# An eleventh 2 MB buffer for expert weights, and the first weight chunk placed between the halves of the first input

## The chip, the cores and the metric

The kernel runs on one core of a Trainium2 chip. The metric is the device time of one execution in microseconds (us), as a median over runs. The engines of the core are named as in the profile: PE (matmul) with its weight load PEld, DVE (vector), ACT (scalar), POOL, and SP, which here issues nearly all DMAs. "PE psum L434" is the matmul helper `mm`, which nearly all products go through.

## What is computed

A stack of three layers on 256 tokens of width 1024, batch 1, all in float32. The part that the change touches is the first layer:

```python
h = _layer_norm(x, ln_in_g, ln_in_b)                 # the first input
mix = _token_mixer(h, w_in, ...)                     # gm_v, gm_u, gates, delta rule, w_pa, w_pb, w_o
h = _layer_norm(ALPHA * h + mix, ln1_g, ln1_b)
ffn = _hier_moe(h, w_rg, b_rg, w_re, b_re, w1, w3, w2)
h = _layer_norm(ALPHA * h + ffn, ln2_g, ln2_b)

def expert_block(xb, e):                             # 32 experts, top 2 of each token
    return (silu(xb @ w1[e]) * (xb @ w3[e])) @ w2[e] # w1, w3: 1024 x 512; w2: 512 x 1024
```

Each of the 96 expert matrices is 2 MB in float32. After the experts come two layers of attention and gated feed-forward (`second_block`), whose code is the same in both kernels.

## The kernel before

**The mixer (from 0 us to about 382 us).** Weights arrive as 2 MB items in slots 0 to 3 of a ring in SBUF. Most products are made exact to about float32 from three passes in a faster format. ACT copies a half of the item (a "chunk", 128x2048) rounded into `mix_hi` (line 1245), DVE subtracts to get the low part (`slot_lo`, line 1808), and PE multiplies high by high, high by low and low by high. The input h is split the same way into `h_hi` (ACT, line 1221) and `h_lo` (DVE, line 1844), in four pieces of two 128-row blocks each. In the first 30 us PE transposes the normalised input (line 540), DVE scales it (line 1839), both are split, and then two products follow on PE: `ab_rows` (24 small products of h with `wab`, 16 rows wide), and `gm_v`, whose first weight item is used in two chunks: chunk 0 needs the blocks 0 to 3 of h, chunk 1 the blocks 4 to 7. PE works through an order written by hand: all 24 products of `ab_rows`, then chunk 0, then chunk 1.

**The delta rule (about 229 us to 310 us).** Between the projections lies a stretch of very small matmuls (64x64), several hundred in a row. SP loads `w_pb` items 0 and 1 ahead of it, at 212 and 229.7 us, and `w_o` at 288.6 and 329.8 us. Between them it waits.

**The experts (about 383 us to 843 us).** PE takes the experts in 16 pairs. A pair reads six items in the order w1, w3 (first expert), w1, w3 (second expert), w2, w2. They are numbered here from 0 to 95 in this order; the table `BUFFER_SLOTS` says where each of ten buffers lies: six are the ring slots, the entries `None` are four pairs of free pages (`spare`). Item u goes to buffer u modulo 10. SP first fills the ten buffers as the places come free (lines 2626 and 2633), then for each u waits until PE has read item u and issues the load of item u + 10 into the same buffer (`consumed` and `load_next`; lines 2652 for pages and 2654 for the ring). That runs as a loop of 30 items taken twice, and 26 items written out. The weights of the next stage (`e_lora`, then three `e_in`, `mla_up`, `e_out`) follow in ring slots in the order of `RING_ORDER`, each when its slot was read for the last time.

**The instruction streams.** PE's expert code is written out, some 11,000 matmuls in the whole program. The profile shows its instructions coming in by DMA on a queue of their own (q8, 79 packets, 1.29 MB).

## Time and profile before

| | us |
|---|---|
| median of 3 runs (lowest to highest) | 1443.21 (1442.02 to 1443.51) |
| the profiled execution, its own time | 1444.03 |
| its span from first to last instruction | 1442.2 |
| PE busy, share of the span | 1391.2, 96% |
| PE waiting for expert weights (DMA ring<-in_w) | 3.7, four times |
| PE waiting for nothing that shows ("issue") | 8.7, four times |

The span is cut by what PE does; PE's busy time counts matmuls as they are pipelined, so a stretch that reads 100% busy can still differ in pace. What matters is therefore when an instruction starts, which the timeline gives, and what ended the idle time ahead of it, which stands in square brackets behind a row. A DMA is known by the time from its issue on SP to its landing.

### The profile page before, as it was taken

What the parts mean: (1) busy time and instruction counts of PE and PEld (TensorE: products, weight loads), DVE (VectorE), ACT (ScalarE), POOL (GpSimd) and SP (SyncE); (2) the same over time, 40 slices, a digit from 0 to 9 for tenths busy, and PEclk for the clock granted to TensorE, in tenths of its full rate; (3) what the DMA queues carried; (4) which work ended last, traced back from release to release, by engine and by line L of the source; (5) the groups of instructions that cost most, each with busy time, mean ns of one, the idle gap of its engine ahead of it and who ended that gap; (6) DMA issues with size and microseconds to landing.
All of it is one profiled execution on the core that took longest, in us unless ns stands there. A gap on an engine that the chain in (4) does not pass through costs nothing.

```text
span 1442.2 us, 25893 instructions
## 1 busy us (share of the span) xinstructions
PE 1391.2 (96%) x11102; PEld 1137.4 (79%) x11102; DVE 703.5 (49%) x1086; ACT 543.1 (38%) x851; POOL 18.6 (1%) x15
## 2 busy tenths in 40 slices
PE   7999999999999999999999979999999998999997
PEld 5999999979666666666656548879999986899996
DVE  6766896346611111111111056866555668755554
ACT  3555773345111111111111144654433456633343
POOL 0000004000000000000000000000000000000000
PEclk9999999899999999999999989999999999999999
DMA  9534432018879999999999991244554631455420
GB/s 388 228 118 176 182 146 85 2 60 339 343 318 426 423 427 423 427 423 427 425 426 424 426 398 67 92 170 178 191 198 165 233 132 45 154 200 187 174 87 30
DMA packets 31473, 351.98 MB, mean 244 GB/s; under 512 B 3088, under 2 KB 3344, under 8 KB 4880
## 3 DMA queue, kind: packets, MB, share of 16 engines
q1 hardware_dynamic: 31232, 349.49, 60.2%
q8 instruction: 79, 1.29, 0.4%
q10 hardware_dynamic: 144, 1.05, 0.2%
q14 instruction: 18, 0.15, 0.0%
HBM read 349.48 MB, written 1.05 MB: 243 GB/s over the span
## 4 chain that ended last, share of the span: by engine, by line
PE 85%; DVE 8%; DMA 3%; ACT 2%; issue 2%; DVEq 0%; ACTq 0%
PE psum L434 83%; DMA ring<-in_w 3%; PE psum L540 1%; DVE slot_lo L1808 1%; ACT pages L1221 1%; PE psum L841 1%; DVE pages L2324 1%; DVE pages L2357 1%; DVE tiny L1756 0%; ACT w_hi L1245 0%; DVE pages L1988 0%; DVE pages L2328 0%; DVE pages L1778 0%; DVE pages L2417 0%; DVE pages L1769 0%
## 5 line engine op out<-in xcount | busy, mean ns | idle before, releaser
L434 PE MATMUL psum<-pages 64*64 64x64 f32 (+11 forms) x3280 | 317.3, 311 | 7.8 <-ACT pages L1221 2.6
L434 PEld LDWEIGHTS psum<-pages 128*64 128x64 f32 (+4 forms) x3280 | 225.4, 151 | 85.1 <-issue 48.0
L434 PE MATMUL psum<-ring,pages 128*64 128x256 f32 (+1 forms) x1556 | 210.2, 423 | 4.2 <-DMA ring<-in_w 3.7
L434 PE MATMUL psum<-x_hi,gu_hi 128*128 128x256 f32 x704 | 199.8, 284 | 0.1
L434 PE MATMUL psum<-x_hi,gu_lo 128*128 128x256 f32 x704 | 199.2, 283 | 0.0
L434 PE MATMUL psum<-x_lo,gu_hi 128*128 128x256 f32 x704 | 199.2, 283 | 0.0
L434 PEld LDWEIGHTS psum<-ring,pages 128*64 128x64 f32 x1556 | 110.8, 137 | 89.3 <-issue 40.9
L434 PEld LDWEIGHTS psum<-x_hi,gu_hi 128*128 128x128 f32 x704 | 134.9, 192 | 2.7 <-issue 0.6
L434 PEld LDWEIGHTS psum<-x_lo,gu_hi 128*128 128x128 f32 x704 | 134.9, 192 | 1.5
L434 PEld LDWEIGHTS psum<-x_hi,gu_lo 128*128 128x128 f32 x704 | 134.9, 192 | 0.0
L1808 DVE TENSOR_TENSOR slot_lo<-ring,mix_hi 128x2048 fp32r<-128x2048 f32 x44 | 100.7, 2290 | 59.1 <-ACT mix_hi L1245 59.0
L2245 DVE SCALAR_TENSOR_TENSOR y_lo<-psum,pages,y_hi 128x512 fp32r<-128x512 f32 x32 | 24.0, 751 | 177.8 <-ACT y_hi L1467 177.8
L434 PE MATMUL psum<-h_hi,mix_hi 128*128 128x256 f32 x448 | 110.6, 287 | 0.0
L434 PE MATMUL psum<-h_lo,mix_hi 128*128 128x256 f32 x448 | 109.5, 284 | 0.0
L2256 DVE TENSOR_TENSOR pages<-pages,psum 128x256 f32<-128x256 f32 x32 | 13.5, 421 | 194.9 <-ACT pages L1476 194.9
L2374 DVE TENSOR_TENSOR gu_lo<-ring,gu_hi 128x2048 fp32r<-128x2048 f32 x44 | 100.9, 2292 | 1.4 <-ACT gu_hi L1575 0.2
L1245 ACT ACTIVATE mix_hi<-ring 128x2048 fp32r<-128x2048 f32 x44 | 84.0, 1912 | 41.3 <-PE psum L434 39.8
L1588 ACT ACTIVATE pages<-pages 128x256 f32<-128x256 f32 x44 | 18.5, 421 | 209.8 <-DVE pages L2391 209.8
L1476 ACT ACTIVATE pages<-psum 128x256 f32<-128x256 f32 x32 | 12.3, 383 | 205.1 <-PE psum L434 205.1
L434 PEld LDWEIGHTS psum<-h_hi,mix_hi 128*128 128x128 f32 x448 | 86.6, 193 | 0.6 <-issue 0.5
L2391 DVE TENSOR_TENSOR pages<-psum,pages 128x256 f32<-128x256 f32 x44 | 18.7, 425 | 139.9 <-PE psum L434 139.9
L434 PEld LDWEIGHTS psum<-h_lo,mix_hi 128*128 128x128 f32 x448 | 86.6, 193 | 0.1
(233 smaller groups left out, 2050.7 us busy)
## 6 DMA issues: line engine op xcount, KB each, us to landing
ring<-in_w SPq DMA_DIRECT2D x58, 2048.0 KB, 25.3
pages<-in_w SPq DMA_DIRECT2D x38, 2048.0 KB, 25.8
ring<-in_ffn SPq DMA_DIRECT2D x44, 1536.0 KB, 6.3
ring<-in_w_in SPq DMA_DIRECT2D x16, 2048.0 KB, 8.5
ring<-in_e_in SPq DMA_DIRECT2D x3, 2048.0 KB, 38.5
ring<-in_w_pa SPq DMA_DIRECT2D x2, 2048.0 KB, 7.7
ring<-in_w_pb SPq DMA_DIRECT2D x2, 2048.0 KB, 8.0
ring<-in_w_o SPq DMA_DIRECT2D x2, 2048.0 KB, 7.4
```

Source lines behind the costliest of these rows:

```text
L434: return pe.matmul(o, lhsT, rhs, start=start, stop=stop, skip_group_check=True)
L540: last = pe.transpose(o[:, j * P:(j + 1) * P], s, ident)
L841: last = pe.transpose(psum[:, 2 + r, c * P:(c + 1) * P], act[:, r, c * P:(c + 1) * P], ident)
L1221: st.do(act_e.activation(o, i, func, **kw), name)
L1245: act_e.activation(high[:, 0:size], slot(n)[:, c * size:(c + 1) * size], ACT.Copy).then_inc(S("w_high"), 1)
L1588: act_e.activation(silu_buf[:, j % 3, :], silu_buf[:, j % 3, :], ACT.Silu).then_inc(S(f"{nm}_silu"), 1)
L1808: ve.tensor_tensor(slot_low[slot_no(n)][:, sl], slot(n)[:, sl], high[:, 0:size], ALU.subtract).then_inc(S("w_split"), 1)
L2245: return ve.scalar_tensor_tensor(y_part["lo"][:, r, :], psum[:, 2 + r, :], gate, y_part["hi"][:, r, :], ALU.mult, ALU.subtract)
L2324: do(ve.scalar_tensor_tensor(e[:, h2, :], bias, slope(g), v[:, 0:SPAN], ALU.mult, ALU.add), f"{sec}s{g}")
L2357: do(ve.tensor_tensor(e[:, :, sl], e[:, :, sl], z[:, :, b].unsqueeze(2).broadcast_to([P, 2, size]), ALU.mult), f"{sec}_probs" if b else None)
L2374: ve.tensor_tensor(gu_part["lo"][j % 2], slot(item_no[(nm, 0)] + j)[:, 0:gu_size], gu_part["hi"][j % 2], ALU.subtract).then_inc(S("gu_spli ...
L2391: ve.tensor_tensor(silu_buf[:, j3, :], psum[:, j3, 0:T], rstd_rows, ALU.mult).then_inc(S("gate_scaled"), 1)
```

## The change

It has three parts. (1) The ring gets a seventh slot, `EXTRA`. It is buffer 0 of now eleven, item 0 is loaded into it right behind `w_pb` item 1, without any wait, and item u + 11 replaces item u. The loop on SP is written out. The space comes from `dynamic_dma_scratch_size=1024` (16384 bytes per partition before). (2) `RING_ORDER` follows the order in which the eleven-buffer scheme lets the ring slots go. (3) At the start PE does half of `ab_rows`, then chunk 0 of `gm_v`, the other half, chunk 1; ACT and DVE split chunk 0 between the second and the third piece of h.

```diff
-BUFFER_SLOTS = (5, None, 2, 3, None, 0, 1, 4, None, None)
+EXTRA = 6
+BUFFER_SLOTS = (EXTRA, 5, None, 2, 3, None, 0, 1, 4, None, None)
-RING_ORDER = (1, 4, 5, 2, 3, 0)
+RING_ORDER = (4, 5, 2, 3, 0, 1)
...
-        ring = sb("ring", [P, SLOTS * SLOT])
+        ring = sb("ring", [P, (SLOTS + 1) * SLOT])
...
-            o = take("ab_rows", 6)
-            for k in range(KD):
-                if k % 2 == 0:
-                    pe.wait_ge(*V("ln_in_low", k // 2 + 1))
-                for n, (wp, xp) in enumerate(PARTS):
-                    last = mm(...)
-            give(last, "ab_rows")
-            project_tokens("gm_v", [("gm_v", 0), ("gm_v", 1)])
+            take("ab_rows", 6)
+            row_products(0)
+            tokens_half("gm_v", 0, ("gm_v", 0), 0, mix_highs[0], h_part)
+            row_products(1)
+            tokens_half("gm_v", 0, ("gm_v", 0), 1, mix_highs[1], h_part)
+            for c in range(2):
+                tokens_half("gm_v", 1, ("gm_v", 1), c, mix_highs[c], h_part)
...
                 act(h_part["hi"][:, sl, :], h_in[:, sl, :], ACT.Copy, "ln_in_high")
+                if i == 1:
+                    split_high(1)
...
             for n, (name, i) in enumerate(items[:moe_first]):
                 load(n, name, i)
+                if phases >= 2 and (name, i) == ("w_pb", 1):
+                    sp.dma_start(ring_slot(EXTRA), first_of(BUFFER_SLOTS.index(EXTRA))).then_inc(landed[EXTRA], 16)
...
-                rounds = (3 * EXPERTS - BUFFERS) // (6 * ROUND)
-                with sp.Fori(0, rounds) as it:
-                    for u in range(6 * ROUND):
-                        consumed(it, u)
-                        load_next(it, u)
-                for u in range(3 * EXPERTS - BUFFERS - 6 * ROUND * rounds):
-                    consumed(rounds, u)
-                    load_next(rounds, u)
+                for u in range(3 * EXPERTS - BUFFERS):
+                    consumed(u)
+                    load_next(u)
...
-    nc = bacc.Bacc("TRN2", target_bir_lowering=False, num_devices=1)
+    nc = bacc.Bacc("TRN2", target_bir_lowering=False, num_devices=1, dynamic_dma_scratch_size=1024)
```

DVE at the start, before: L1829 normalises the input, L1839 scales a transposed piece, L1844 makes its low part, L1808 the low part of a weight chunk.

```order
L1839 TENSOR_SCALAR pages<-psum,consts 128x256 x4
L1844 TENSOR_TENSOR h_lo<-pages,h_hi 128x512
L1839 TENSOR_SCALAR pages<-psum,consts 128x256 x2
L1844 TENSOR_TENSOR h_lo<-pages,h_hi 128x512
L1839 TENSOR_SCALAR pages<-psum,consts 128x256 x2
L1844 TENSOR_TENSOR h_lo<-pages,h_hi 128x512 x2
L1808 TENSOR_TENSOR slot_lo_61<-ring,mix_hi 128x2048 x2
```

DVE at the start, of the changed kernel, where L1852, L1859 and L1821 are the same three statements.

```order
L1852 TENSOR_SCALAR pages<-psum,consts 128x256 x4
L1859 TENSOR_TENSOR h_lo<-pages,h_hi 128x512 x2
L1852 TENSOR_SCALAR pages<-psum,consts 128x256 x4
L1821 TENSOR_TENSOR slot_lo_61<-ring,mix_hi 128x2048
L1859 TENSOR_TENSOR h_lo<-pages,h_hi 128x512 x2
L1821 TENSOR_TENSOR slot_lo_61<-ring,mix_hi 128x2048
```

The low part of chunk 0 moved ahead of the low parts of the last two pieces of h, and the second piece's low part ahead of the third piece's scaling.

PE at the same place, as a piece of the difference: the rows with a plus stood ahead of all weight products and now follow chunk 0 (the three shown, four times).

```order
 L434 MATMUL psum<-mix_hi,h_lo 128x512
 L434 MATMUL psum<-slot_lo_61,h_hi 128x512 x8
+L434 MATMUL psum<-h_hi,wab_hi 16x256
+L434 MATMUL psum<-h_lo,wab_hi 16x256
+L434 MATMUL psum<-h_hi,wab_lo 16x256
```

Half of the small products now stand behind the sixteen high and eight low products of chunk 0.

SP from the delta rule into the first expert loads, before.

```order
L2602 DMA ring<-in_w_pb 128x4096 x2
L2602 DMA ring<-in_w_o 128x4096 x2
L2616 DMA pages<-in_router 128x864
L2617 DMA pages<-in_ln 128x2048
L2633 DMA ring<-in_w 128x4096
L2626 DMA pages<-in_w 128x4096
```

SP at the same place, of the changed kernel; L2623 is the load into `EXTRA`.

```order
L2617 DMA ring<-in_w_pb 128x4096 x2
L2623 DMA ring<-in_w 128x4096
L2617 DMA ring<-in_w_o 128x4096 x2
L2634 DMA pages<-in_router 128x864
L2635 DMA pages<-in_ln 128x2048
L2652 DMA ring<-in_w 128x4096
L2645 DMA pages<-in_w 128x4096
```

One 2 MB load was added between `w_pb` and `w_o`; every later expert load stands at its old place and carries the next item.

## Rows read from the trace of the kernel before

**Rows 1.** The page: busy tenths of the DMA engines in 40 slices

```profile
DMA  9534432018879999999999991244554631455420
```

**Rows 2.** Busy time by stretch: us, PE, PEld, DVE, ACT, POOL, PEclk, DMA share, GB/s

```profile
398.20:404.20 6.00, 6.00 (x57) 4.69 (x58) 1.10 (x5) 2.16 (x3) 0.00 (x0) 1.00 0.01 3
450.00:600.00 150.00, 150.00 (x1169) 92.21 (x1168) 19.16 (x39) 22.55 (x45) 0.00 (x0) 1.00 1.01 425
```

**Rows 3.** Timeline of PE, experts: start us, us, engine, line, op, operands, count [idle <-releaser]

```profile
755.80 7.08 PE L434 MATMUL psum<-pages 128*64 128x256 f32 x64
...
769.73 0.73 PE L434 MATMUL psum<-y_hi,spots 64*128 64x512 f32 x4
...
783.15 3.62 PE L434 MATMUL psum<-pages 128*64 128x256 f32 x32
...
799.15 0.73 PE L434 MATMUL psum<-y_hi,spots 64*128 64x512 f32 x4
...
812.57 3.62 PE L434 MATMUL psum<-ring,pages 128*64 128x256 f32 x32
...
820.62 3.67 PE L434 MATMUL psum<-ring,pages 128*64 128x256 f32 x32 [0.97 <-DMA ring<-in_w]
825.42 3.67 PE L434 MATMUL psum<-ring,pages 128*64 128x256 f32 x32 [1.12 <-DMA ring<-in_w]
829.02 0.73 PE L434 MATMUL psum<-y_hi,spots 64*128 64x512 f32 x4
```

**Rows 4.** Timeline of PE, the start

```profile
13.02 0.37 PE L434 MATMUL psum<-h_hi,wab_hi 128*16 128x256 f32 x1
...
15.40 0.28 PE L434 MATMUL psum<-h_hi,wab_lo 128*16 128x256 f32 x1
...
16.07 0.28 PE L434 MATMUL psum<-h_lo,wab_hi 128*16 128x256 f32 x1
16.19 0.28 PE L434 MATMUL psum<-h_hi,wab_lo 128*16 128x256 f32 x1
...
17.81 0.50 PE L434 MATMUL psum<-mix_hi,h_hi 128*128 128x512 f32 x1 [0.20 <-ACT mix_hi L1245]
...
21.57 1.98 PE L434 MATMUL psum<-slot_lo,h_hi 128*128 128x512 f32 x8
23.39 0.39 PE L434 MATMUL psum<-mix_hi,h_hi 128*128 128x512 f32 x1
```

**Rows 5.** Timeline of DVE, the start

```profile
12.20 0.68 DVE L1844 TENSOR_TENSOR h_lo<-pages,h_hi 128x512 fp32r<-128x512 f32 x1
12.79 0.99 DVE L1839 TENSOR_SCALAR pages<-psum,consts 128x256 f32<-128x256 f32 x2
...
17.79 2.29 DVE L1808 TENSOR_TENSOR slot_lo<-ring,mix_hi 128x2048 fp32r<-128x2048 f32 x1 [1.11 <-ACT mix_hi L1245]
```

**Rows 6.** Timeline of ACT, the start

```profile
12.31 0.63 ACT L1221 ACTIVATE h_hi<-pages 128x512 fp32r<-128x512 f32 x1 [0.27 <-DVE pages L1839]
...
15.86 3.71 ACT L1245 ACTIVATE mix_hi<-ring 128x2048 fp32r<-128x2048 f32 x2
```

**Rows 7.** Line L2602 in the window 2.5 to 3.0 us: the first weight item, issued at 2.60

```profile
DMA to landing us min/median/max: 9.3/9.3/9.3
```

**Rows 8.** Timeline of PE, small matmuls of the delta rule

```profile
238.51 15.47 PE L434 MATMUL psum<-pages 64*64 64x64 f32 x507 [1.36 <-issue]
```

**Rows 9.** DMA issue of the window 229.7 to 230.0 us: KB, us to landing

```profile
ring<-in_w_pb SPq DMA_DIRECT2D x1, 2048.0 KB, 8.5
```

**Rows 10.** DMA packets by queue, window 236.2 to 236.3 us: packets, MB, share

```profile
q8 instruction: 1, 0.02, 59.6%
```

**Rows 11.** DMA packets by queue, window 239.6 to 239.8 us

```profile
q8 instruction: 1, 0.02, 38.2%
```

**Rows 12.** DMA packets by queue, window 239.6 to 255.5 us

```profile
q8 instruction: 5, 0.08, 2.5%
```

**Rows 13.** DMA issue of the window 798.7 to 799.0 us: KB, us to landing

```profile
ring<-in_e_lora SPq DMA_DIRECT2D x1, 1792.0 KB, 40.9
```

More of the change, by code:

```diff
@@ L254, in build @@
         free = [S(f"bank{b}_free") for b in range(8)]
-        landed = [S(f"slot{s}_landed") for s in range(SLOTS)]
+        landed = [S(f"slot{s}_landed") for s in range(SLOTS + 1)]
         by_page = pages[:].rearrange("p (n c) -> p n c", c=PAGE)
-        spare = {1: by_page[:, 5:7, :], 4: by_page[:, 2:5:2, :], 8: by_page[:, 1:4:2, :], 9: by_page[:, 7:13:5, :]}
+        spare = {2: by_page[:, 5:7, :], 5: by_page[:, 2:5:2, :], 9: by_page[:, 1:4:2, :], 10: by_page[:, 7:13:5, :]}
         spare_landed = {b: S(f"spare{b}_landed") for b in spare}
@@ L574, in _, with row_products @@
             pe.wait_ge(*V("wab_split", 1))
-            o = take("ab_rows", 6)
-            for k in range(KD):
-                if k % 2 == 0:
-                    pe.wait_ge(*V("ln_in_low", k // 2 + 1))
-                for n, (wp, xp) in enumerate(PARTS):
-                    last = mm(o[0:16, 0:T], wab_part[wp][:, k, :], h_part[xp][:, k, :], k == 0 and n == 0, k == KD - 1 and n == 2)
-            give(last, "ab_rows")
-            project_tokens("gm_v", [("gm_v", 0), ("gm_v", 1)])
+            take("ab_rows", 6)
+            def row_products(half):
+                o = bank_of("ab_rows")
+                for k in range(half * KD // 2, (half + 1) * KD // 2):
+                    if k % 2 == 0:
+                        pe.wait_ge(*V("ln_in_low", k // 2 + 1))
+                    for n, (wp, xp) in enumerate(PARTS):
+                        last = mm(o[0:16, 0:T], wab_part[wp][:, k, :], h_part[xp][:, k, :], k == 0 and n == 0, k == KD - 1 and n == 2)
+                if half:
+                    give(last, "ab_rows")
+            row_products(0)
[4 more added lines that the diff above has]
+                tokens_half("gm_v", 1, ("gm_v", 1), c, mix_highs[c], h_part)
             pe.wait_ge(*evacuated("ab_rows"))
@@ L1834, in _ @@
                "wab_split")
-            for i in range(5):
-                if i < 4:
+            for first in (0, 2):
+                for i in (first, first + 1):
                     v = await_full(ve, f"ln_in_T{i}")
@@ L1840, in _ @@
                                             ALU.mult, ALU.add), f"ln_in_T{i}" if k % 2 else None)
-                if i:
-                    sl = slice(2 * i - 2, 2 * i)
-                    ve.wait_ge(*V("ln_in_high", i))
+                if first:
+                    split_low(1)
+                for i in (first, first + 1):
+                    sl = slice(2 * i, 2 * i + 2)
+                    ve.wait_ge(*V("ln_in_high", i + 1))
                     do(ve.tensor_tensor(h_part["lo"][:, sl, :], h_in[:, sl, :], h_part["hi"][:, sl, :], ALU.subtract), "ln_in_low")
@@ L2618, in _ @@
             if phases >= 2:
-                first_of = lambda i: io[LOADS[i % 6]][2 * (i // 6) + LOAD_OF[i % 6]]
                 halves_of = lambda src: src.rearrange("p (n c) -> p n c", c=PAGE)
-                spare_free = {1: V("h_split", 8), 4: (full[place["w_pb3"][0]], place["w_pb3"][1]),
-                              8: (full[place["w_o3"][0]], place["w_o3"][1]), 9: V("ln1_tokens", 4)}
+                spare_free = {2: V("h_split", 8), 5: (full[place["w_pb3"][0]], place["w_pb3"][1]),
+                              9: (full[place["w_o3"][0]], place["w_o3"][1]), 10: V("ln1_tokens", 4)}
                 for i, s in enumerate(BUFFER_SLOTS):
+                    if s == EXTRA:
+                        continue
                     if s is None:
@@ L2634, in _, with consumed, load_next @@
                 base = place["moe_base"]
[L2636 removed]
+                def consumed(u):
                     x = u % 6
                     if x in (0, 2):
[L2640 removed]
+                        sp.wait_ge(*V("w1_read", 2 * (u // 6) + x // 2 + 1))
                     elif x < 4:
[L2642 removed]
+                        sp.wait_ge(full[x // 2], u // 6 + base[x // 2] + 1)
                     else:
[L2644 to L2650 removed]
+                        sp.wait_ge(full[x - 2], 2 * (u // 6) + base[x - 2] + 2)
+                def load_next(u):
+                    b, src = u % BUFFERS, first_of(u + BUFFERS)
                     if b in spare:
```

10 lines of the change are left out of this document (1 added, 9 removed).

## The prediction

> **What bounds the kernel now.** I read the page first, then the expert stage in the windows and in PE's timeline, then the start, then the quiet stretch into which the new load falls. The page shows that the DMA engines are nearly full at the very start and from the tenth slice on (about 325 us) to the twenty-fourth, and idle elsewhere [rows 1]. In the expert stage they move 425 GB/s at a share of 1.01, so they can give no more [rows 2]. A pair of experts needs six items, 12.58 MB, which take 29.6 us at that rate. PE needs less: the h products of one pair start at 755.80 and those of the next at 783.15, 27.35 us later [rows 3]. So the weights fall behind PE by 2.2 us with each pair, and the ten items that lie ready at the start are a lead that is used up. It lasts until the last two pairs. There PE waits four times, 0.97 and 1.12 us in the last pair [rows 3] and twice in the pair ahead of it. The true loss is read from starts, since each stop also costs a little refill: from the first h product to the first scatter it is 13.93 us in an undisturbed pair (755.80 to 769.73), 16.00 in the next to last (783.15 to 799.15) and 16.45 in the last (812.57 to 829.02) [rows 3]. Excess: 2.07 + 2.52 = **4.6 us**. Outside the experts PE works nearly without a gap, so time comes only from gaps in PE's row.
>
> **Part 1, the eleventh buffer, as a lead.** Item u + 11 is now issued at the moment at which item u + 10 was, since SP waits for the same read of item u; and the places in which the first fill goes come free in the same order. From 398.2 to 404.2 us the DMA engines stand still, the ten buffers being full, and then they never stop [rows 2]; that gap stays. So in the saturated stretch each item lands when its predecessor did: 2.097 MB / 425 GB/s = 4.93 us earlier; the two waits of the last pair end 4.80 us apart (820.62 and 825.42), and I go by that [rows 3]. Item 93 is the tightest. It lands when item 92 did, at about 820.6. Without any waits PE would want it at 825.42 less the delay gathered by then, 2.07 + 2.52 less the small rest behind it, about 4.5, so at 820.9. It is there with 0.3 us to spare, the other three with more than 1.5. All four waits go, and nothing else is late next: the two w2 items of the last pair have 1.5 us or more. **-4.55 us**, taken between -3.2 (item 93 still late by up to 1.3 us, should the stream run 0.3% slower over 430 us) and -4.6. The loads of the next stage: `RING_ORDER` gives `e_in` and `mla_up` ring slots that PE lets go up to one product block later than before, but `e_lora`, issued at 798.7, landed only 40.9 us later [rows 13], the queue ahead of it being that long. They wait in the queue, not for their slot, and the queue is 4.9 us earlier while PE is 4.55 us earlier. Cost nothing. The written-out loop issues the same DMAs on an SP that only waits. Nothing.
>
> **Part 2, the load into `EXTRA`.** It is free of any wait and needed 150 us later. Its DMA queue is empty until `w_o` at 288.6. But PE is not indifferent here. `w_pb` item 1 is issued at 229.73 and lands 8.5 us later, at 238.3 [rows 9]; behind it come 507 matmuls of 64x64 in 15.47 us, 30.5 ns each, ahead of which PE stood for 1.36 us and waited for nothing that shows [rows 8]. What shows beside it is an instruction packet of 16 KB, which starts at 236.2 to 236.3, while `w_pb` flows [rows 10]. The next one starts at 239.6 to 239.8, five of them lie in 15.9 us, so one each 3.9 us when the data queue is quiet, and PE has no such gap then [rows 11, 12]. Take 3.9 us of PE's own time back from 239.7, with the 1.36 us of standing between: the packet at 236.2 was due at about 239.7 - 3.9 - 1.36 = 234.4. It came 1.8 us late, behind data packets, and PE has about 0.45 us of slack for it. So a small-matmul stretch stalls by 1.36 us when an instruction packet meets a 2 MB transfer. Now the transfer of `EXTRA` follows at once and keeps the engines full for 4.9 us more, to about 242. The packet of 239.7 falls into it. The nearest row is the stall itself: once more **+1.4 us**. A little more is likely, because the packet of 236.2 came when its engine had just run out of `w_pb` data, and now there is more behind: half a data packet, 0.3 us. Together **+1.7 us**. Bounds: 0 if a fetch passes the data (then the first stall would be of another cause), and 4.9 us if a fetch waits for the whole second transfer. The path there is PE's own, so what is lost stays lost.
>
> The Trainium skill bears on this twice. "Runtime: NRT & Kernel Launch", Instruction fetch mechanics, says that each engine refills 256 instructions (16 KiB) at a time by its own DMA queue and calls the cost mostly hidden; the trace agrees on the size (q8) and not on the rest, as the 1.36 us show. By that page the term would be 0 and the time 1437.9. "DMA: Bandwidth & Descriptors", Queues, rings and completion order, says that a DMA engine goes round its rings but drains some 9 to 17 descriptors from one before it moves on. If the upper figure held, the fetch would wait through both transfers; that is rival C below, worked out from rows.
>
> **Part 3, the start.** PE needs 4.79 us from the first `ab_rows` product (13.02) to the first weight product (17.81) [rows 4]. The first twelve products start 0.22 us apart (13.02 to 15.40), the later ones 0.12 (16.07, 16.19) [rows 4]. Without waits that is 12 x 0.21 + 12 x 0.12 = 3.9 us; the rest, **0.9 us**, is waiting for pieces of h and for ACT's copy. After: ACT has the second `h_hi` at 12.94, and the weights landed at 2.60 + 9.3 = 11.9 [rows 6, 7], so chunk 0's copy takes 12.94 to 14.8 (half of 3.71). DVE does the two first low parts to 13.7 (0.68 each), then four scalings to 15.6 (0.99 a pair), then chunk 0's low part to 17.9 (2.29), the last low parts to 19.2 and chunk 1's to 21.4 [rows 5]. PE: twelve products to 15.5; chunk 0's sixteen high products from 15.5 to 19.3 (17.81 to 21.57 took 3.76) and eight low ones to 21.1 (1.82) [rows 4]; twelve products, for which h is ready since 19.2, to 22.5; then chunk 1. Before, the same work was done at 23.39 [rows 4]. No wait is left, the closest being the copy at 14.8 for 15.5. **-0.9 us**; bounds -0.9 (there is no more waiting to remove) and 0 (if PE's quick pace, which begins at 15.3, comes later with the new order). DVE and ACT are ahead of their old place afterwards, so nothing is pushed on.
>
> **Sum.** -4.55 + 1.7 - 0.9 = -3.75 us. On the profiled execution 1444.03 - 3.75 = 1440.3 (span 1442.2 to 1438.4); it is 0.8 us above the median, so the median should be 1443.2 - 3.75 = **1439.5**. About 0.2%, 2.9 us, is what a measurement of this kernel can tell from no change; the bound is 1440.3.
>
> **Rivals.** A, the forecast: 1438.7 to 1440.9 with its small spreads. B, the second stall does not come or is under 0.5 us: 1443.2 - 5.45 + 0.25 = 1438.0. For it: in the expert stage, where the DMA is always full, no such stall shows; against: there the matmuls are ten times as long, so a block of instructions lasts some 16 us. C, the fetch waits for all of `EXTRA`: +4.9 in place of 1.7, 1442.7. Against it: the packet at 236.2 waited for 1.8 us of the 4.9 of a transfer. D, the lead is not worth its whole: item 93 late, or the start brings nothing: -3.2 + 1.7 - 0.3, 1441.4. E, the other side, slower: the scratch of 1024 bytes holds the DMA queue's descriptors, and a sixteenth of it lets only one transfer be under way at a time. Then each of 85 streamed items would take its lone time, 8.5 us [rows 9], where it takes 4.93; the price is 85 x 3.6 = 300 us, less the lead of 36, some 1700 us. It decides as soon as fewer than two transfers fit; with two or more the stream stays at 425 GB/s and costs nothing. Against it: all data packets are marked hardware_dynamic. The Trainium skill, the same DMA page, SWDGE vs HWDGE vs iDMA, places only the software rings in that scratch; no run here shows it yet.
>
> **How the numbers follow.** Chances: A 0.52, B 0.20, C 0.12, D 0.13, E 0.03. The forecast is A's 1439.5. Its own range is 1438.7 to 1440.9; with B below, C and D above, I go from 1437.6 to 1442.4, which leaves out E and the far ends of B and C. Faster by over 0.2% (under 1440.3): three quarters of A and all of B, some 0.60. Within 0.2%: the rest of A, C and D, 0.37. Slower: 0.03.
>
> **What would show it.** In the profile after: no PE wait on ring<-in_w (else part 1's lead is short); the last two pairs 13.9 us each from h to scatter; PE's first product of chunk 1 at about 22.5 in place of 23.39; an "issue" wait near 237 and a second one near 241 to 243, where before there was one, the second of 1.0 to 2.0 us. If the second is missing, B; if one of them is 5 us, C. Landings of expert weights that are 7 us or more apart would be E. The sum fails most easily in the size of part 2, whose two bounds are 4.9 us apart.

## The result and the profile after

The changed kernel takes **1436.75 us** (median of 5 runs, 1436.45 to 1438.11). The kernel before, run beside it, takes 1443.51 us (median of 5, 1442.02 to 1445.24). The ratio is 0.9956, 95% interval 0.9945 to 0.9967. That is 6.8 us faster, where 3.75 us was forecast, and 0.85 us below the lower end of the range. Two more measurements of the same changed kernel (experiments, below) gave ratios of 0.9957 and 0.9963. Over all its 15 runs the changed kernel has a mean of 1437.5 us, and the kernel before over the 62 runs that stood beside these and the other kernels one of 1443.1 us: **5.6 us**, give or take 0.6. So the sign is certain, and the size is best taken from the many runs: the first medians, 6.8 us apart, are partly luck. The profiled execution of the changed kernel took 1436.71 us, with a span of 1434.9 us.

I go through the profile after in the order of the prediction. **The experts** first. Timeline of PE, changed kernel (start us, us, engine, line, operation, operands, count):

```profile
767.18 0.73 PE L434 MATMUL psum<-y_hi,spots 64*128 64x512 f32 x4
...
794.51 0.73 PE L434 MATMUL psum<-y_hi,spots 64*128 64x512 f32 x4
...
807.93 3.62 PE L434 MATMUL psum<-pages 128*64 128x256 f32 x32
...
821.84 0.73 PE L434 MATMUL psum<-y_hi,spots 64*128 64x512 f32 x4
```

The brackets "<-DMA ring<-in_w" of [rows 3] are gone, and the last pair takes 13.91 us from its first h product to its first scatter (807.93 to 821.84), as an undisturbed one did before. The last three scatters start 27.33 us apart (767.18, 794.51, 821.84), which is PE's own pace for a pair, where the last pair of before took 29.87 (799.15 to 829.02) and the one ahead of it 29.42. From the first scatter to the last it is 410.02 us, and it was 414.66. The stream itself is what it was, 426 GB/s for 425 in [rows 2]:

```profile
450.00:600.00 150.00, 150.00 (x1174) 92.13 (x1172) 19.17 (x39) 21.41 (x43) 0.00 (x0) 1.00 1.01 426
```

**The small products** of the delta rule, the place of [rows 8]. Timeline of PE, changed kernel:

```profile
228.27 7.52 PE L434 MATMUL psum<-pages 64*64 64x64 f32 x246
237.42 3.94 PE L434 MATMUL psum<-pages 64*64 64x64 f32 x127 [1.63 <-issue]
242.63 16.32 PE L434 MATMUL psum<-pages 64*64 64x64 f32 x523 [1.27 <-issue]
258.88 1.12 PE L434 MATMUL psum<-consts 128*128 128x512 f32 x2
```

Of the kernel before, the first product of the same stretch and the first one behind it:

```profile
229.63 7.52 PE L434 MATMUL psum<-pages 64*64 64x64 f32 x246
...
258.60 1.12 PE L434 MATMUL psum<-consts 128*128 128x512 f32 x2
```

There are two stalls for which nothing is waited, 1.63 and 1.27 us, where before there was one of 1.36 (and a small one of 0.17 further on). The second one is new. The brackets are not the whole loss. By starts, the 896 products take 28.97 us before (229.63 to 258.60) and 30.61 after (228.27 to 258.88): 1.64 us more, where the brackets differ by 1.37. An instruction packet shows beside each: q8 in the windows 234.9 to 235.1 and 240.2 to 240.4 of the changed kernel (packets, MB, share), to be laid beside [rows 10, 11].

```profile
q8 instruction: 1, 0.02, 29.8%
```

```profile
q8 instruction: 1, 0.02, 30.4%
```

Both fall into the two transfers, issued at 228.4 and 228.7. Issues of the window 228 to 229 us, KB and us to landing, which answer to [rows 9]:

```profile
ring<-in_w_pb SPq DMA_DIRECT2D x1, 2048.0 KB, 8.7
ring<-in_w SPq DMA_DIRECT2D x1, 2048.0 KB, 13.0
```

**The start**, the place of [rows 4 to 6]. Timelines of PE, and of DVE, changed kernel:

```profile
12.93 0.37 PE L434 MATMUL psum<-h_hi,wab_hi 128*16 128x256 f32 x1
...
14.59 0.34 PE L434 MATMUL psum<-h_hi,wab_lo 128*16 128x256 f32 x1
14.77 0.28 PE L434 MATMUL psum<-h_hi,wab_hi 128*16 128x256 f32 x1
...
15.12 0.40 PE L434 MATMUL psum<-mix_hi,h_hi 128*128 128x512 f32 x1
...
20.61 0.28 PE L434 MATMUL psum<-h_hi,wab_hi 128*16 128x256 f32 x1
...
22.01 0.40 PE L434 MATMUL psum<-mix_hi,h_hi 128*128 128x512 f32 x1
```

```profile
15.30 2.28 DVE L1821 TENSOR_TENSOR slot_lo<-ring,mix_hi 128x2048 fp32r<-128x2048 f32 x1
17.50 1.29 DVE L1859 TENSOR_TENSOR h_lo<-pages,h_hi 128x512 fp32r<-128x512 f32 x2
18.71 2.29 DVE L1821 TENSOR_TENSOR slot_lo<-ring,mix_hi 128x2048 fp32r<-128x2048 f32 x1
```

No bracket is left in PE's row from its first product on. Its first product of chunk 1 starts at 22.01; it was 23.39. DVE's low parts are done at 17.6, 18.8 and 21.0, each ahead of its reader.

**What I had not looked for: the granted clock.** Windows of both kernels around two short stretches (us, PE, PEld, DVE, ACT, POOL, PEclk, DMA share, GB/s). Of the kernel before:

```profile
262.00:284.00 22.00, 20.57 (x182) 19.74 (x179) 6.67 (x8) 8.43 (x18) 0.00 (x0) 0.77 0.01 1
383.00:400.00 17.00, 17.00 (x100) 12.36 (x97) 8.37 (x56) 2.43 (x6) 2.31 (x3) 0.90 0.77 323
```

Of the changed kernel:

```profile
262.00:284.00 22.00, 20.57 (x197) 19.84 (x192) 6.96 (x8) 9.48 (x21) 0.00 (x0) 0.84 0.01 1
383.00:400.00 17.00, 17.00 (x111) 12.44 (x112) 9.09 (x59) 3.06 (x6) 2.31 (x3) 1.00 0.70 295
```

The seventh number behind the window is the granted clock, 1.00 being 2.4 GHz. A mean of 0.77 over 22 us is 10.2 us at half of it, 1.2 GHz (2 x 0.23 x 22); 0.84 is 6.8 us, and 0.90 over 17 us is 3.4 us. So the profiled execution of before ran 3.4 us longer at 1.2 GHz near 268 us, and 3.4 us near 387 us where the changed one had none. PE's timeline prices them. The 40 router products, before and after:

```profile
383.39 8.87 PE L434 MATMUL psum<-pages 128*128 128x36 f32 x40
```

```profile
382.32 7.17 PE L434 MATMUL psum<-pages 128*128 128x36 f32 x40
```

Near 268 us, 32 products of the delta rule's second part, before and after, and the first product with a low part behind them:

```profile
268.51 7.35 PE L434 MATMUL psum<-pages 64*128 64x128 f32 x32 [1.43 <-ACT pages L1221]
...
280.74 2.08 PE L434 MATMUL psum<-h_hi,slot_lo 128*128 128x256 f32 x16
```

```profile
268.79 5.62 PE L434 MATMUL psum<-pages 64*128 64x128 f32 x32 [1.43 <-ACT pages L1232]
...
279.67 2.08 PE L434 MATMUL psum<-h_hi,slot_lo 128*128 128x256 f32 x16
```

The same work takes 12.23 us in the one (268.51 to 280.74) and 10.88 in the other. What PE did before its clock fell: near 268 it ran 128 small products and stood 1.43 us for ACT (the clock fell during that wait before, at 267.9, and behind it after, at 270.7); near 387 it had stood 1.38 and 0.23 us for DVE between transposes, and it did so in both kernels, though the clock fell in one alone.

**The account** of the two profiled executions, between marks of PE and SP that both traces have. The parts add up to the difference of the spans, 1442.2 - 1434.9 = 7.3 us.

| stretch | before | after | difference |
|---|---|---|---|
| to the issue of `w_pb` item 1 (start moved) | 229.73 | 228.37 | -1.36 |
| the 896 small products, first start to the next product's | 28.97 | 30.61 | +1.64 |
| rest of the way to the issue of `w_o` item 1 (clock near 268) | 71.11 | 69.76 | -1.35 |
| from there to the first scatter (clock near 387) | 84.55 | 83.08 | -1.47 |
| first to last scatter (experts) | 414.66 | 410.02 | -4.64 |
| behind the last scatter | 613.22 | 613.08 | -0.14 |

Three rows are the prediction's three terms, and they sum to -4.36. Two more, -2.8 us together, lie where the clock differs, and the first of them is just what the work near 268 lost above (12.23 - 10.88 = 1.35).

### The profile page after: what moved, and what is told of

Its sections match the earlier page's. It is cut to its first block, busy times and chain, and to the rows that moved or that the text cites. A ratio compares the mean times of both kernels' runs of the same rounds, so it can differ in the third digit from the quotient of the medians.

```text
span 1434.9 us, 25774 instructions
## 1 busy us (share of the span) xinstructions
PE 1386.7 (97%) x11102; PEld 1135.5 (79%) x11102; DVE 703.5 (49%) x1086; ACT 543.0 (38%) x851; POOL 18.6 (1%) x15
## 4 chain that ended last, share of the span: by engine, by line
PE 89%; DVE 7%; ACT 2%; issue 1%; DMA 0%; DVEq 0%; ACTq 0%
PE psum L434 86%; PE psum L540 2%; DVE slot_lo L1821 1%; PE psum L852 1%; ACT pages L1232 1%; DVE pages L2339 1%; DVE pages L2372 1%; DVE tiny L1769 0%; DVE pages L2003 0%; DVE pages L2343 0%; DVE pages L1791 0%; DVE pages L2432 0%; DVE pages L1782 0%; DVE pages L2382 0%; ACT w_hi L1256 0%
## 5 line engine op out<-in xcount | busy, mean ns | idle before, releaser
L434 PE MATMUL psum<-pages 64*64 64x64 f32 (+9 forms) x3184 | 299.9, 305 | 8.8 <-issue 2.9
L434 PEld LDWEIGHTS psum<-pages 128*64 128x64 f32 (+3 forms) x3184 | 216.8, 151 | 78.3 <-issue 44.2
L434 PE MATMUL psum<-ring,pages 128*64 128x256 f32 (+1 forms) x1652 | 223.2, 424 | 0.9 <-ACT pages L1492 0.9
L434 PEld LDWEIGHTS psum<-ring,pages 128*64 128x64 f32 x1652 | 117.1, 137 | 92.0 <-issue 42.6
L1821 DVE TENSOR_TENSOR slot_lo<-ring,mix_hi 128x2048 fp32r<-128x2048 f32 x44 | 100.8, 2290 | 57.4 <-ACT mix_hi L1256 57.3
L1489 ACT ACTIVATE pages<-psum 128x256 f32<-128x256 f32 x32 | 12.3, 383 | 200.4 <-PE psum L434 200.4
```

The source lines that it names most:

```text
L434: return pe.matmul(o, lhsT, rhs, start=start, stop=stop, skip_group_check=True)
L1821: ve.tensor_tensor(slot_low[slot_no(n)][:, sl], slot(n)[:, sl], high[:, 0:size], ALU.subtract).then_inc(S("w_split"), 1)
```

## Theories, and the experiments

Theory: the three parts are worth about -1.4 us (the start), -4.6 (the buffer) and +1.3 to +1.7 (its load) each by itself and add up to between -4.7 and -4.3. What is measured beyond that is the clock's stretches at 1.2 GHz, which vary between executions of one kernel. Rivals: (1) the rest of the gain is a fourth effect of the change (the scratch of 1024 bytes, the written-out loop, `RING_ORDER`); (2) the stall among the small products is of that place in the code, and the transfer only stands beside it; (3) the missing stretch at 387 us is the change's doing.

### The start alone

The reorder of `ab_rows` and `gm_v` and of DVE's and ACT's pieces, with ten buffers:

```diff
-            project_tokens("gm_v", [("gm_v", 0), ("gm_v", 1)])
+            row_products(0)
+            tokens_half("gm_v", 0, ("gm_v", 0), 0, mix_highs[0], h_part)
+            row_products(1)
...
```

> The kernel before with the new order at the start alone (ten buffers, old loop on SP). Theory (the start is worth what PE's row shows, and the rest of the gain beyond the sum came from half-clock windows): PE's first w_pb release moves from 229.7 to about 228.4 us, the four DMA waits at the end of the experts stay (excess 4.6 us over undisturbed pairs), one issue wait of about 1.4 us near 236, total about -1.4 us, 1442.1. Rival (the start also brings the other 3 us, for instance because PE reaches the later stretches at a luckier moment for the clock): the windows of granted clock 0.5 near 268 and 387 us shrink or go here too and the total is -3 to -4 us.

Measured: 1441.64 us (median of 11), ratio 0.9987 (0.9978 to 0.9996). `w_pb` item 1 is issued at 228.09, the four DMA waits of the last two pairs are there (0.53, 1.12, 1.06 and 1.14 us), and there is one stall by issue, 1.73 us. So the start is worth 1.3 to 1.8 us of time (difference of medians, of means), where I had 0.9; the reason stands in the next section. And this kernel, with ten buffers, has no stretch at 1.2 GHz near 387 us. Rival 3 loses its ground as far as the buffer is meant: the stretch goes without it too.

### The buffer alone

The eleventh buffer, its load behind `w_pb` item 1, the new `RING_ORDER`, the written-out loop and the scratch of 1024 bytes, with the old start:

```diff
-BUFFER_SLOTS = (5, None, 2, 3, None, 0, 1, 4, None, None)
+EXTRA = 6
+BUFFER_SLOTS = (EXTRA, 5, None, 2, 3, None, 0, 1, 4, None, None)
...
```

> The changed kernel with the old order at the start. Theory: no DMA wait in the experts, each pair 27.33 us (-4.6 us), two issue waits in the small matmuls, the first about 1.5 and the second about 1.3 us later (+1.5 us), total about -3.1 us, 1440.4, give or take 1.5 us of half-clock windows whose place is chance. Rival (the buffer part gave the surplus of 3 us, by shortening the half-clock windows near 268 and 387 us): -5 to -6 us, and these windows are shorter here than in the kernel before.

Measured: 1438.86 us (median of 5), ratio 0.9966 (0.9952 to 0.9979). No DMA wait in the experts; first to last scatter 410.02 us. The two stalls are there:

```profile
229.61 7.52 PE L434 MATMUL psum<-pages 64*64 64x64 f32 x246
238.21 3.94 PE L434 MATMUL psum<-pages 64*64 64x64 f32 x127 [1.08 <-issue]
243.69 15.71 PE L434 MATMUL psum<-pages 64*64 64x64 f32 x523 [1.54 <-issue]
```

The lead and the second stall belong to the buffer, and neither needs the new start. The time is 4.1 us lower by medians (5.1 by means). Theory had 3.1 and the rival 5 to 6, so the time alone favours neither, and it is more than the -4.6 + 1.3 = -3.3 of its rows; this profiled execution also lacks the stretch near 387 us and one near 940 us, while its 10.2 us near 268 are not shorter.

### `EXTRA` loaded one item earlier

The changed kernel with the load of `EXTRA` behind the earlier `w_pb` item, issued near 210 us, where PE does larger products:

```diff
-                if phases >= 2 and (name, i) == ("w_pb", 1):
+                if phases >= 2 and (name, i) == ("w_pb", 0):
```

> The changed kernel with the load into the seventh slot issued behind the first w_pb item (about 210 us) instead of behind the second (about 229 us), so its transfer is over before the 64x64 matmuls begin. Theory (an instruction packet that meets a data transfer comes late and stalls PE there): the second issue wait (1.27 us in the changed kernel) is gone, the first falls from 1.63 to about 1.36; total -1.3 to -1.6 us against the changed kernel, 1435.3. Rival (the waits belong to places in PE's instruction stream, whatever the DMA does): both waits stay and the time is that of the changed kernel, 1436.7.

Measured: 1436.21 us (median of 5), ratio 0.9952 (0.9938 to 0.9966). Timeline of PE:

```profile
228.79 6.89 PE L434 MATMUL psum<-pages 64*64 64x64 f32 x226
237.03 19.44 PE L434 MATMUL psum<-pages 64*64 64x64 f32 x650 [1.35 <-issue]
256.40 1.13 PE L434 MATMUL psum<-consts 128*128 128x512 f32 x2
```

The second stall is gone with the transfer, and the 650 products run through. At its new place, under products of other shapes, the same 2 MB cost PE no stall. The first stall, beside `w_pb` item 1, stays; that it came out at the 1.36 expected is luck, for it is 1.08 to 1.73 in the other profiles. The time alone does not decide: 1436.21 lies nearer to the rival's 1436.7 than to 1435.3, and by means it is 1.1 us below the changed kernel, with an uncertainty of 1.2.

### Both transfers out of the small products

As the last one, and SP also holds `w_pb` item 1 back until the 64x64 products of the delta rule's first part are done:

```diff
+                if (name, i) == ("w_pb", 1):
+                    b_, n_ = place["uc0"]
+                    sp.wait_ge(full[b_], n_)
                 load(n, name, i)
```

> As the one with the early load, and the second w_pb item is held back on SP until the first large product after the 64x64 matmuls (about 258 us), so no data flows during them at all. Theory: no issue wait over 0.2 us is left between 225 and 258 us; -2.9 us against the changed kernel, 1433.8. The w_pb item lands by about 267 us and is wanted after 310, so nothing else waits. Rival (places in the instruction stream): a wait of 1.4 us near 235 us stays. Second rival (the clock takes it back: a denser stretch of small matmuls ends earlier and a half-clock window of 3.4 us more falls on work): the issue waits go but the total falls by less than 1.5 us.

Measured: 1433.24 us (median of 5), ratio 0.9932 (0.9918 to 0.9945). It is the fastest version. Timeline of PE:

```profile
228.79 26.55 PE L434 MATMUL psum<-pages 64*64 64x64 f32 x889
255.27 1.12 PE L434 MATMUL psum<-consts 128*128 128x512 f32 x2
```

889 products in one piece, at 29.9 ns each, with no stall; nobody waits for the late `w_pb`, issued at 257.45.

The same version once more:

> The version with both loads out of the small products once more. The rows that do not vary give -1.5 at the start, -4.6 in the experts and -1.4 of stalls, -7.5 us: 1435.7. The first run gave 1433.24. If the difference was chance, this one lies nearer 1435; if it belongs to the kernels with eleven buffers, it is 1433 to 1434 again.

Measured: 1433.97 us (median of 5), ratio 0.9939 (0.9925 to 0.9953), and again no stall by issue. So 1433 to 1434 us is the version's own time, some 3.7 us below the changed kernel by the means of 10 and 15 runs (1433.8 and 1437.5). The two stalls are 2.7 us together by their brackets (mean of three profiles). Read from starts, they are worth all of it: the stretch of 896 small products takes 30.61, 30.71 and 29.90 us in the three profiles of the changed kernel and 26.71 and 26.66 in the two of this one, 3.7 us less. The 1 us that the brackets lack lies right beside the stalls and in smaller gaps further on, some 127 products apart.

### `w_pb` late, with ten buffers

The kernel before with that one wait of SP's and nothing else:

> The kernel before, ten buffers, with w_pb item 1 held back until the last 64x64 products of the delta rule's first part are done; nothing else is changed. Theory (an instruction packet that meets a 2 MB transfer is what makes PE stand): no stall by issue between 230 and 260 us in the profile, four DMA waits in the last two pairs as before, and 1443.2 - 1.4 = 1441.8. Rival (the stall belongs to that place in the code, and the transfer only stands beside it): a stall of 1.1 to 1.7 us near 238 us all the same, and 1443.2. Second rival (the late w_pb is worth more than the stall, as the row of the version with both suggested): below 1441.0.

Measured: 1441.06 us (median of 11), beside 1442.65 of before; ratio 0.9993 (0.9984 to 1.0002). Timeline of PE:

```profile
229.37 26.72 PE L434 MATMUL psum<-pages 64*64 64x64 f32 x896
...
816.82 3.67 PE L434 MATMUL psum<-ring,pages 128*64 128x256 f32 x32 [1.17 <-DMA ring<-in_w]
821.61 3.67 PE L434 MATMUL psum<-ring,pages 128*64 128x256 f32 x32 [1.12 <-DMA ring<-in_w]
```

The first stall, which stands in every profile with `w_pb` at its old place, is gone, so rival 2 falls: without the transfer the place alone makes no stall. Half of it is true, though. In all ten profiles with a transfer in this stretch the first stall comes behind exactly 246 products, and in the five with two transfers the second comes 127 products further on. So it takes both: a certain place in PE's instruction stream, and a transfer under way when PE reaches it. The instruction packets say what comes between. The one ahead of the first stall starts 3.7 to 4.4 us behind the first small product in the three profiles without a transfer and 6.2 to 6.9 us behind it in the ten with one, and PE goes on 2.25 to 2.44 us after the packet's start in all 15 stalls. That is as close as the traces come to showing that PE stands for its instructions.

The time moved by -1.1 us (means) to -1.6 (medians), where 1.4 was forecast; by starts the stretch is 2 us shorter (26.65 us, 28.97 and 28.41 in the two profiles of before). The ratio's interval reaches from 2.3 us faster to 0.3 us slower, so it holds both and also no change. The second rival's bound of 1441.0 was missed by 0.06 us, which decides nothing. Three of the four DMA waits show, and the experts take their 414.62 us as before.

### One more load, never read

The kernel before with a seventh ring slot and, behind `w_pb` item 1, one more 2 MB load into it; nothing waits for it and nothing reads it:

```diff
+                if (name, i) == ("w_pb", 1):
+                    sp.dma_start(ring_slot(SLOTS), io["w1"][0]).then_inc(S("unused_landed"), 16)
```

> The kernel before, ten buffers and old start, plus one 2 MB load behind the second w_pb item into a seventh slot that nobody reads (scratch of 1024 bytes to make room). It measures the cost of that transfer by itself. Theory (fetch against data): a second issue wait of 1.2 to 1.6 us about 5 us behind the first, nothing gained, the four DMA waits in the experts stay: +1.5 us, 1444.4. Rival (the second wait came with the other parts of the change): one wait only, 1442.9.

Measured: 1444.12 us (median of 11), ratio 1.0005 (0.9996 to 1.0014), +1.0 us by medians, +1.1 by means. Timeline of PE:

```profile
229.53 7.52 PE L434 MATMUL psum<-pages 64*64 64x64 f32 x246
238.23 3.94 PE L434 MATMUL psum<-pages 64*64 64x64 f32 x127 [1.18 <-issue]
243.44 15.76 PE L434 MATMUL psum<-pages 64*64 64x64 f32 x523 [1.27 <-issue]
```

A transfer that no engine waits for makes the second stall. That is the disputed cost by itself: 1.27 us in the row, and the time, 1.0 us for the 1.5 forecast, agrees within what the runs can tell.

### Scratch and loop alone

The kernel before with the scratch of 1024 bytes and the written-out loop of expert loads:

> The kernel before with only the scratch of 1024 bytes and SP's loop written out; still ten buffers, six slots, old start. Theory: neither does anything: 1442.9, landings of expert weights 4.9 us apart, four DMA waits at the end. Rival (a small part of the surplus comes from here, through fewer register instructions on SP or a smaller scratch): -0.5 to -2 us, seen as a shorter gap of the DMA engines near 400 us or a quicker stream.

Measured: 1442.67 us (median of 11), ratio 0.9996 (0.9987 to 1.0005). The experts take 414.38 us, as with the old loop. Rival E is out, and so is rival 1 as far as these two are meant; `RING_ORDER` has no run of its own. The Trainium skill, "DMA: Bandwidth & Descriptors", SWDGE vs HWDGE vs iDMA, places only the software rings in that scratch; by that rule, this run agrees.

### The same kernels again, for the clock

The changed kernel a second and a third time, and the kernel before again:

> The changed kernel once more, for a second profile and more times. Theory (3 us of the gain of the first pair of profiles lay in half-clock windows whose number is chance): issue waits (1.6 and 1.3 us), start and pairs of 27.33 us come out the same to 0.1 us apart from the issue waits' own 0.3, while the windows of granted clock 0.5 come out different in number, in steps of 3.4 us, and the median moves by up to 1.5 us. Rival (the change itself shortens them): again 6.8 us near 270 and none near 387.

> The changed kernel itself once more, for the 1.3 us that are left between the sum of the rows that do not vary (-4.6 us) and the measured gain (-5.8 to -6.3). If the rest is chance in the windows of half clock, the median of this run lies nearer 1438.6 and its windows of granted clock 0.5 add up to 27 us or more; if the rest belongs to the kernel, it is 1437.4 or less with any windows.

> The kernel before once more, for a second profile. Theory (chance): the window near 387 us (3.4 us at half clock, some 1.5 us lost) is missing or elsewhere, and that near 268 is 6.8 or 10.2 us. Rival (the kernel's own): both are there as in the first profile, 10.2 and 3.4 us.

Measured: changed 1436.98 us, ratio 0.9957 (0.9943 to 0.9970), and 1437.78 us, ratio 0.9963 (0.9950 to 0.9977); before again 1443.18 us, ratio 1.0002 (0.9993 to 1.0011). Windows near 268 us, changed kernel the second time, and near 387 us, before again:

```profile
262.00:284.00 22.00, 20.57 (x178) 19.74 (x175) 6.61 (x8) 8.27 (x18) 0.00 (x0) 0.77 0.01 1
```

```profile
383.00:400.00 17.00, 17.00 (x97) 12.28 (x98) 8.48 (x58) 2.23 (x6) 2.31 (x3) 0.90 0.73 308
```

The first says that the same program has 6.8 us at 1.2 GHz near 268 in one execution (0.84 above) and 10.2 in another (0.77), so there it is chance. The second is the rival's row: the kernel before has its 10.2 us near 268 and its 3.4 near 387 again. The third run of the changed kernel was to decide between 1438.6 (chance) and 1437.4 or less (the kernel's own), and its 1437.78 lies between them: it did not. The table sets all profiles side by side; times at half clock are read from the granted clock's record, the rest from starts in the traces. "Stalls" are the brackets of 0.15 us and more, and "small" is the whole stretch of 896 small products by starts. "Late" is what follows the last scatter, and the clock there the one of the stretch from 1190 to 1225 us.

| kernel | `w_pb` 0 issued | stalls | small | half clock near 268 | near 387 | `w_o` 1 to first scatter | experts | half clock near 1200 | late |
|---|---|---|---|---|---|---|---|---|---|
| before | 211.98 | 1.53 | 28.97 | 10.2 | 3.4 | 84.55 | 414.66 | 3.4 | 613.22 |
| before again | 211.84 | 1.08 | 28.41 | 10.2 | 3.4 | 84.55 | 414.49 | 6.8 | 614.56 |
| scratch and loop | 211.88 | 1.73 | 29.09 | 10.2 | 0 | 83.08 | 414.38 | 6.8 | 615.03 |
| unused load | 211.89 | 2.45 | 29.60 | 6.8 | 0 | 83.07 | 414.67 | 6.8 | 615.08 |
| `w_pb` late, ten buffers | 211.73 | 0 | 26.65 | 10.2 | 0 | 83.07 | 414.62 | 0 | 612.76 |
| start only | 210.32 | 1.73 | 28.95 | 6.8 | 0 | 83.08 | 414.83 | 6.8 | 615.15 |
| buffer only | 211.97 | 2.62 | 29.73 | 10.2 | 0 | 83.08 | 410.02 | 3.4 | 611.21 |
| changed | 210.61 | 2.90 | 30.61 | 6.8 | 0 | 83.08 | 410.02 | 3.4 | 613.08 |
| changed, second | 210.18 | 2.72 | 30.71 | 10.2 | 0 | 83.07 | 410.00 | 6.8 | 614.79 |
| changed, third | 210.20 | 2.35 | 29.90 | 10.2 | 0 | 83.07 | 410.01 | 3.4 | 613.69 |
| `EXTRA` early | 210.51 | 1.35 | 28.24 | 10.2 | 0 | 83.08 | 410.01 | 3.4 | 613.43 |
| both out | 210.92 | 0 | 26.71 | 6.8 | 0 | 83.08 | 410.02 | 3.4 | 613.21 |
| both out, second | 210.34 | 0 | 26.66 | 10.2 | 0 | 83.06 | 410.01 | 0 | 613.38 |

Four columns follow the edit: the issue of `w_pb` item 0 (211.7 to 212.0 with the old start, 210.2 to 210.9 with the new), the stalls, the small products (26.7 with no transfer beside them, 28.2 to 29.1 with one, 29.6 to 30.7 with two), and the experts (414.4 to 414.8 with ten buffers, 410.0 with eleven). The clock's columns follow no edit closely. 6.8 us near 1200 goes with a late part of 614.6 to 615.2 us, whichever the kernel; 3.4 or none with 611.2 to 613.7. 3.4 us near 387 goes with 84.55, none with 83.06 to 83.08.

**What stays open.** The stretch near 387 showed in both profiles of the kernel before and in none of the other eleven, four of them with the old ten buffers. And 6.8 us near 1200 showed in four of six profiles with ten buffers, in one of seven with eleven. So on average the clock may favour the changed kernel a little, by chance or because its work reaches these places at another moment. One profile in five to eleven runs cannot settle that.

Each run has a mean granted clock on record, and two things can be read from these. Within a kernel the time follows it: over 147 runs of the nine versions the correlation is -0.76 (the lower the clock, the longer the run), and 0.001 of mean clock goes with 0.6 us. So the scatter from run to run is in good part the clock's. But the mean over the changed kernel's 15 runs, 0.9889, is no higher than the 0.9895 over 68 runs of the kernel before. The change does not give PE more of the quick clock in all; at most the slow stretches fall where they cost less (near 840 us they last 6.8 or 10.2 us with ten buffers, and up to 13.7 with eleven). I leave it open.

## Why the prediction was wrong in its number

**What bounds the kernel** was read rightly. The four DMA waits went, nothing was late next, the stream kept its rate, and the item I held for the tightest was no trouble. Term of part 1: -4.55 forecast; the rows gave -4.64 in the first pair of profiles, and 410.0 for 414.4 to 414.8 in all.

**Part 2** was right in mechanism. A second stall came where it was put, "near 237 and a second one near 241 to 243", one experiment moved it away by moving the transfer alone (`EXTRA` early), a second by moving both, and one made it with an unread load. Its size was right by starts: 1.7 us forecast; 1.7 measured between the three profiles of the changed kernel (30.4 us in the mean) and the two of before (28.7), and 1.4 between all five profiles with two transfers and all five with one. The reason I gave for the last 0.3 us was luck, though. The second bracket itself is no longer than the first (0.7 to 1.5 us, where the half data packet asked for more than 1.4); the rest lies beside the brackets, as the prediction had allowed for in the experts ("the true loss is read from starts") and not here. Nor was the packet of 236.2 late by 1.8 us with 0.45 us of slack: against the profiles without a transfer it was late by 2.6, and PE could bear 1.2 of it. The bound of 4.9, rival C, is refuted: the packet of 240.3 held PE for 1.27 us, not for the whole transfer, and rival B is too. Of the Trainium skill's rules that I weighed, the page "Runtime: NRT & Kernel Launch", Instruction fetch mechanics, has the fetch mostly hidden; the rows disagree for this one kind of stretch, by 0.7 to 1.7 us each time, and agree with it in the experts, where PE has no gap over 0.02 us from 400 to 780 us in the profile of before.

**Part 3** is the mis-sized term on the good side: -0.9 forecast, -1.4 measured (-1.38 at the first product of chunk 1, 23.39 to 22.01; -1.44 in the mean issue of `w_pb` item 0, 211.88 with the old start and 210.44 with the new). The failed step is the bound "there is no more waiting to remove", and under it "12 x 0.21 + 12 x 0.12": I took the slow pace of the first products, and its end at 15.3 us, from one execution as the kernel's own. It isn't. In the kernel with scratch and loop alone, whose order at the start is the old one, the first products came 0.11 to 0.12 us apart from the beginning, and what this gained was lost again in waiting for DVE; timeline of PE:

```profile
14.35 0.29 PE L434 MATMUL psum<-h_hi,wab_hi 128*16 128x256 f32 x1 [0.57 <-DVE h_lo L1844]
...
15.86 0.29 PE L434 MATMUL psum<-h_hi,wab_hi 128*16 128x256 f32 x1 [0.63 <-DVE h_lo L1844]
```

In the new order PE has its data, and a quick pace counts. In the first profile of the changed kernel nine starts were slow (12.93 to 14.59), in its third none; timeline of PE of the third:

```profile
12.80 0.27 PE L434 MATMUL psum<-h_hi,wab_hi 128*16 128x256 f32 x1 [0.23 <-DVE h_lo L1859]
12.91 0.28 PE L434 MATMUL psum<-h_lo,wab_hi 128*16 128x256 f32 x1
...
21.59 0.40 PE L434 MATMUL psum<-mix_hi,h_hi 128*128 128x512 f32 x1
```

There chunk 1 begins at 21.59, 0.42 us ahead of the first profile's 22.01, of which 0.13 lies ahead of the first product. Counted from its own first product, PE reaches chunk 1 in 10.33 to 10.40 us in all six profiles with the old order, slow start or not, and in 8.75 to 8.80 in six of the seven with the new one; only the first profile of the changed kernel, with its nine slow starts, took 9.08. So the old order's waits had hidden PE's pace, and the new one shows it where the slow start is long: the term is -1.6 us as a rule and -1.3 in the pair of profiles that was to be explained. (The issue of `w_pb` item 0 shows 1.44, since PE's first product itself starts 0.1 us later in the mean of the profiles with the new order.) The line's own sum also comes to 4.0 and not 3.9, which leaves 0.8 us of waiting.

So the steady terms add up to -4.6 + 1.7 - 1.4 = -4.3 us, in place of -3.75 (-4.7 if the second transfer is taken by its bracket). **The step that put the time out of the range** is another: the line "its own range is 1438.7 to 1440.9" had no term for what varies between executions, and the start's term failed by the same fault. I corrected the profile for its distance from the median (0.8 us) and took every other row of it as the kernel's own. PE's stretches at 1.2 GHz near 268 and 387 us stood in that trace, each 3.4 us of them worth 1.35 to 1.5 us of path, and I had not looked at the granted clock by stretch outside the experts. By the steady rows alone the time would have been 1443.2 - 4.3 = 1438.9, inside the range. Of the 6.8 us between the first medians 4.3 are steady rows; of the rest, 1.2 is the scatter of two medians of five runs (the many runs say 5.6), and 1.3, with an uncertainty of 0.6, remains, about as large as a single such stretch is worth. In the table this rest lies in the two columns where the slow stretches differ: from `w_o` item 1 to the first scatter, and late. That it is the clock is argued from them and not shown, since no run held the clock fixed and the mean granted clock is no higher with the change. The cause of this last part stays open.

Three smaller slips changed nothing. With no second stall the time would have been 1443.2 - 4.55 - 0.9 = 1437.8, not 1437.9. The products of the experts take 0.13 us each in the mean (150 us for 1169 in [rows 2]) and the small ones 0.03, so they are four times as long, not ten. And the base of 1443.2 came from three runs, where the many give 1443.1.

## What to carry to other kernels

Before a term is summed against one profiled execution, read the granted clock of every short stretch on the path, in that execution and where possible in a second, and give the range a term for each stretch that may come or not. A free place in the DMA queue is not free for PE where PE runs through instructions of 30 ns each: put large transfers under long instructions, and where that isn't possible charge each of them with the loss already seen, read from starts and not from the bracket (here 2.1 us for the first and 1.4 for the second). A lead of one buffer is worth the waits it covers and no more, so read its gain from starts of a disturbed group against an undisturbed one.

## What the runs showed of the hardware

- An instruction packet of 16 KB that meets a 2 MB transfer came late enough to stop PE for 0.7 to 1.7 us among 64x64 products (ten profiles, one stall for each transfer in that stretch, always at the same product, each ended 2.25 to 2.44 us after the start of a packet that came some 2.6 us late for the first stall), and not under larger products, where `EXTRA` was put in one experiment. By starts 896 such products take 26.7 us with no transfer beside them, 28.7 with one and 30.1 with two. With both transfers out of that stretch no stall is left, and that is the fastest version, 1433.2 and 1434.0 us.
- PE's clock falls to 1.2 GHz for 3.4 to 13.7 us at the same few places of the program, and how long differs between executions of the same kernel. On the path 3.4 us of it cost 1.35 us (near 268) and 1.47 us (near 387), and the runs of one kernel spread over 4 to 5 us in eleven runs (the one before from 1440.8 to 1444.9), with a correlation of -0.76 to their mean granted clock.
- PE's first products of 128x256 start 0.21 us apart in some executions, for none up to eleven of them, and 0.11 to 0.12 in the rest. The two paces are those that products of the same size have at 1.2 and at 2.4 GHz later in the trace, as the timeline of PE of the kernel before shows inside the stretch at half clock (the first two) and behind it (the last two). The record of the granted clock agrees where it exists. In the profile of before its first entry is at 15.30 us, at 1.00, and the first quick start is at 15.40; in all ten profiles that have slow starts, these end at the record's first entry, to within one product, and in the three where it stands at 11.9 to 12.3 us, ahead of PE's first product, none is slow. A view of an earlier window prints 1.00 for want of an entry, so there the pace of the products tells more than the view.

```profile
276.38 0.41 PE L434 MATMUL psum<-h_hi,mix_hi 128*128 128x256 f32 x1
276.60 0.41 PE L434 MATMUL psum<-h_lo,mix_hi 128*128 128x256 f32 x1
...
280.38 0.28 PE L434 MATMUL psum<-h_lo,mix_hi 128*128 128x256 f32 x1
280.50 0.28 PE L434 MATMUL psum<-h_hi,mix_hi 128*128 128x256 f32 x1
```

- DMAs issued by SP lost nothing with a scratch of 1024 bytes: 0.9996 (0.9987 to 1.0005).
